# Applying the norm weights inside the high/low split of x, and squaring x on ScalarE

## The chip, the cores and the metric

The kernel runs on one core of a Trainium2 chip. The metric is the device time of one execution in microseconds (us); the median of the runs is compared.

## The reference

One inference step of a decoder with two layers, for 256 prompt tokens and 8 x 8 sample tokens (320 tokens in all, D = 1024, F = 2816). Each layer is

```
x = x + 0.5 * SwiGLU_1(rms(x))
h = rms(x); z = h @ w_in                     # 40 blocks of 128 columns
A, B = two kinds of windowed attention over z and the caches
x = x + (sigmoid(gA) * (A @ w_branch_a) + sigmoid(gB) * (B @ w_branch_b)) @ w_out
x = x + 0.5 * SwiGLU_2(rms(x))

def _rms(x, g):
    y = x * rsqrt(mean(x * x, axis=-1) + 1e-6)
    return y * g
```

and a last `_rms` follows the second layer. So there are seven norms: six in front of matrix products and one at the end. Everything is float32; the outputs are y and the new K/V window buffers.

## The kernel before, in words

**Layout.** Activations lie transposed: 128 partitions by 320 tokens, and x has KD = 8 such chunks. A weight comes as a *unit*, 128 x 1024 floats (8 tiles of 128 x 128); there are 208 units in a layer.

**Precision.** Every float32 product is made of three matrix products. An operand is split in a high part (rounded to fp32r) and a low part (operand minus high part): `product()` (L635 to L641) issues `hi*whi`, `lo*whi`, `hi*wlo`. ScalarE makes `whi` with a Copy (L973, `round_unit`), VectorE makes `wlo` with a subtraction (L1146, `rest_unit`). The rings `raw`, `whi` and `wlo` hold four units each; SyncE loads a unit into `raw` when the `wlo` that used the slot four units earlier is done.

**Norm.** The products take x times the norm's weights, and 1/rms is multiplied in behind them. For each of the 8 chunks of x:

1. VectorE, `add_to_x` (L1174): adds the result of the matrix product in PSUM to the chunk; it signals `taken`.
2. VectorE, `scale_x` (L1160): `xg = x * gain`, a tensor_scalar into one of two buffers `xg`; it signals `xg_ready`.
3. ScalarE, `round_x` (L985): `xhi = Copy(xg)`; it signals `xhi_done`.
4. VectorE, `rest_x` (L1165): `xlo = xg - xhi`; it signals `xs_ready`, on which TensorE waits chunk by chunk.
5. GpSimd, `add_squares` (L1407, L1409): `sq = x * x`, `ssq = ssq + sq`.

When all 8 are summed, TensorE adds over the partitions with a matrix of ones (`sum_squares`, L646), ScalarE takes the root (L978, which needs a table load), VectorE the reciprocal (L1170).

**Order around it.** The order is written out by hand, engine by engine; every engine runs its own instructions strictly in that order, and semaphores join them. There are four places with such chunks:

- the *start*, where x comes in four transfers with the first four weight units between them (L1367 to L1379 for VectorE);
- the *down* stages of the four FFNs, where a chunk of x is finished once in four units (`down` in `ffn_vec`, `ffn_act`; `ffn_pool`);
- the *w_out* stage of the two mixers, where a chunk is finished with every unit (last loops of `mixer_vec`, `mixer_act`, `mixer_pool`); there, TensorE writes to two banks in turn and may start unit m when the sum into x of unit m - 2 is `taken`;
- behind each of them `first_units` (L648 to L664): TensorE multiplies two new units side by side with chunks 0 to 6, and `sum_squares` stands in it behind the tenth product (chunk 2 of the second unit); chunk 7 of both comes last.

In the w_out stage VectorE's loop for unit m is

```
dve.wait_ge(unit_used, L * NU + U_WO + m + RING + 1)
add_to_x(L, BK_WO + m % 2, m, R_WO + m, 1.0)
scale_x(L * 3 + 2, m, m % 2)
rest_unit(L, U_WO + 4, 0, 0, m, UT)
rest_x(L * 3 + 2, m, m % 2)
```

The buffers `xg` and `sq` serve the mixer too (as `zs` and `sh`), at other times.

Of the kernel before, what the change touches and what calls it, by code (L numbers as in the profile page):

```python
# [13 lines left out]
P = 128  # L14
# [258 lines left out]
def build(nc, a):  # L273
    ctx = ExitStack()
    with ctx:
# [13 lines left out]
        xg = sb("xg", [P, 2, TOK])  # L289
        xhi = sb("xhi", [P, KD, TOK], F32R)  # L290
        xlo = sb("xlo", [P, KD, TOK], F32R)
        sq = sb("sq", [P, TOK])
# [48 lines left out]
        zs, sh = xg, sq  # L341
# [18 lines left out]
        xg_ready = sem("xg_ready")  # L360
# [607 lines left out]
        def _(act):  # L968
# [11 lines left out]

            def round_x(norm, m, slot):

                act.wait_ge(xg_ready, norm * KD + m + 1)
                dst = xhi[:, m, :] if isinstance(m, int) else xhi[:, at(m), :].rearrange("p o n -> p (o n)")
                nc.scalar.activation(dst, xg[:, slot, :], ACT.Copy).then_inc(xhi_done, 1)  # L985

            def ffn_act(L, f):
# [32 lines left out]
            def mixer_act(L):  # L1020
# [121 lines left out]
        def _(dve):  # L1142
# [16 lines left out]
            def scale_x(norm, m, slot):  # L1159
                nc.vector.tensor_scalar(xg[:, slot, :], chunk(x, m), gain(norm, m), None, ALU.mult)\  # L1160
                    .then_inc(xg_ready, 1)

            def rest_x(norm, m, slot):
                dve.wait_ge(xhi_done, norm * KD + m + 1)
                nc.vector.tensor_tensor(chunk(xlo, m), xg[:, slot, :], chunk(xhi, m).bitcast(F32), ALU.subtract)\  # L1165
                    .then_inc(xs_ready, 1)
# [11 lines left out]
            def ffn_vec(L, f):  # L1178
# [12 lines left out]
                def down(i, tail):  # L1191
                    norm = L * 3 + 1 + 2 * f
                    for o in range(2):
                        for s in range(4):
                            if s == 3:
                                dve.wait_ge(unit_used, L * NU + i * 8 + U_DN[f] + 4 * o + s + RING + 1)
                                add_to_x(L, BK_DN + o, i * 2 + o, i * 2 + R_DN[f] + o, 0.5)
                                scale_x(norm, i * 2 + o, o)
                            rest_unit(L, U_DN[f] + 4, i, 8, 4 * o + s,
                                      UT if o == 1 and tail == "next" else DN_TILES[s])  # L1200
                        rest_x(norm, i * 2 + o, o)
# [9 lines left out]
            def mixer_vec(L):  # L1211
# [158 lines left out]
            scale_x(0, 0, 0)  # L1370
            for m in range(KD):
                if m + 1 < KD:
                    dve.wait_ge(x_in[(m + 1) * XPARTS // KD], 16)
                    if m >= 1:
                        dve.wait_ge(xs_ready, m)
                    scale_x(0, m + 1, (m + 1) % 2)
# [180 lines left out]
```

## Time and profile before

| | |
|---|---|
| median of 3 runs | 1560.98 us (1560.46 to 1568.88) |
| profiled execution, first to last instruction | span 1556.9 us |
| busy: PE / DVE / ACT / POOL | 97% / 57% / 42% / 27% |
| chain that ended last | PE 87%, issue 4%, DVE 3%, DMA 3%, POOL 2%, ACT 1% |
| mean granted TensorE clock | 0.995 |

The profile gives the profiled execution by its span alone; the median of the runs stands 4.1 us above it. PE is TensorE, DVE VectorE, ACT ScalarE, POOL GpSimd. In a timeline a row is start, duration, engine, line, operation, output and inputs, shape and, in brackets, how long the engine had been idle and what ended that. A matmul's duration is its latency; how fast matmuls follow each other is read from their starts.

### The profile page before, as it was taken

How to read it: one execution, taken by the hardware profiler on the slowest of the kernel's cores; microseconds unless marked ns; L12 is line 12 of the kernel's file. 1: busy time of each engine (PE TensorE's matmuls, PEld its weight loads, DVE VectorE, ACT ScalarE, POOL GpSimd, SP SyncE). 2: the span in 40 equal slices, each digit the busy share in tenths (PEclk: the TensorE clock that was granted, in tenths of full speed). 3: DMA queues.
4: the chain of work that ended last, by engine and by line, in shares of the span. 5: the costliest groups of instructions: out<-in, count | busy, mean ns of one | idle time of the engine just before them, and what ended most of it. 6: DMA issues, size and time to landing. Idle time of an engine off the chain costs nothing.

```text
span 1556.9 us, 33517 instructions
## 1 busy us (share of the span) xinstructions
PE 1504.6 (97%) x11346; PEld 1425.1 (92%) x11346; DVE 883.5 (57%) x1383; ACT 656.7 (42%) x1123; POOL 414.7 (27%) x415
## 2 busy tenths in 40 slices
PE   6999999999999899999999999999999989999996
PEld 5999999988768899999999999999877689999996
DVE  7555567854334765555655455677534258545566
ACT  4444334455343344433344443355544344444333
POOL 5222223211113432222232222232111053322221
PEclk9999999999999999999999999999999999999998
DMA  7885565767685588646688846666776746985464
GB/s 283 323 298 187 169 202 192 254 205 246 216 283 170 175 312 295 217 149 187 203 307 296 287 141 190 206 222 206 244 254 228 244 139 219 326 303 160 145 202 159
DMA packets 95290, 352.11 MB, mean 226 GB/s; under 512 B 12368, under 2 KB 23888, under 8 KB 92496
## 3 DMA queue, kind: packets, MB, share of 16 engines
q1 hardware_dynamic: 95184, 350.77, 67.8%
q8 instruction: 58, 0.95, 0.2%
q14 instruction: 48, 0.39, 0.1%
HBM read 345.61 MB, written 94.37 MB: 283 GB/s over the span
## 4 chain that ended last, share of the span: by engine, by line
PE 87%; issue 4%; DVE 3%; DMA 3%; POOL 2%; ACT 1%; DVEq 0%; SPq 0%; POOLq 0%; ACTq 0%
PE ps L639 27%; PE ps L641 26%; PE ps L640 26%; PE ps L864 2%; DMA kvc<-in_kcache 2%; PE ps L850 2%; POOL ma L1460 1%; PE ps L723 1%; DMA kvc<-in_vcache 1%; DVE xlo L1165 1%; PE ps L791 1%; PE ps L758 1%; DVE wlo L1146 1%; PE ps L715 1%; DVE x L1174 0%
## 5 line engine op out<-in xcount | busy, mean ns | idle before, releaser
L1146 DVE TENSOR_TENSOR wlo<-raw,whi 128x1024 fp32r<-128x1024 f32 (+2 forms) x420 | 520.4, 1240 | 446.5 <-ACT whi L973 445.4
L639 PE MATMUL ps<-xhi,whi 128*128 128x320 f32 x2048 | 647.6, 316 | 16.3 <-DVE wlo L1146 8.4
L641 PE MATMUL ps<-xhi,wlo 128*128 128x320 f32 x2048 | 635.0, 310 | 0.0
L640 PE MATMUL ps<-xlo,whi 128*128 128x320 f32 x2048 | 634.8, 310 | 0.0
L973 ACT ACTIVATE whi<-raw 128x1024 fp32r<-128x1024 f32 (+2 forms) x420 | 403.8, 964 | 301.4 <-PE ps L641 301.2
L639 PEld LDWEIGHTS ps<-xhi,whi 128*128 128x128 f32 x2048 | 386.0, 188 | 39.2 <-issue 27.2
L640 PEld LDWEIGHTS ps<-xlo,whi 128*128 128x128 f32 x2048 | 386.6, 189 | 0.6 <-issue 0.2
L641 PEld LDWEIGHTS ps<-xhi,wlo 128*128 128x128 f32 x2048 | 386.4, 189 | 0.0
L641 PE MATMUL ps<-act_hi,wlo 128*128 128x320 f32 x704 | 217.6, 309 | 0.0
L639 PE MATMUL ps<-act_hi,whi 128*128 128x320 f32 x704 | 217.6, 309 | 0.0
L640 PE MATMUL ps<-act_lo,whi 128*128 128x320 f32 x704 | 217.6, 309 | 0.0
L1416 POOL TENSOR_TENSOR up_s<-gate_s,up_s 128x320 f32<-128x320 f32 x88 | 85.9, 976 | 379.6 <-DVE up_s L1187 379.6
L640 PEld LDWEIGHTS ps<-act_lo,whi 128*128 128x128 f32 x704 | 132.2, 188 | 0.0
L639 PEld LDWEIGHTS ps<-act_hi,whi 128*128 128x128 f32 x704 | 132.1, 188 | 0.0
L641 PEld LDWEIGHTS ps<-act_hi,wlo 128*128 128x128 f32 x704 | 132.1, 188 | 0.0
L1407 POOL TENSOR_TENSOR sq<-x 128x320 f32 (+1 forms) x56 | 44.7, 798 | 278.9 <-DVE x L1174 274.8
L1455 POOL TENSOR_TENSOR t<-xg,rinv 128x320 f32<-128x320 f32 x46 | 41.3, 897 | 261.8 <-ACT xg L1032 261.8
L994 ACT ACTIVATE gate_s<-gate_s 128x320 f32<-128x320 f32 x88 | 41.4, 470 | 164.0 <-DVE gate_s L1187 164.0
L1420 POOL TENSOR_TENSOR act_lo<-up_s,act_hi 128x320 f32 x88 | 86.5, 983 | 70.0 <-ACT act_hi L1002 70.0
L1032 ACT ACTIVATE xg<-ps 128x320 f32<-128x320 f32 x80 | 34.7, 434 | 142.8 <-PE ps L641 142.8
L1187 DVE TENSOR_TENSOR gate_s<-ps,rinv 128x320 f32<-128x320 f32 x88 | 43.2, 491 | 86.5 <-PE ps L641 85.9
L1064 ACT ACTIVATE e<-e,nmx 128x128 f32<-128x128 f32 (+5 forms) x60 | 32.9, 549 | 96.9 <-DVE nmx L1313 96.9
(123 smaller groups left out, 1362.7 us busy)
## 6 DMA issues: line engine op xcount, KB each, us to landing
out_new_a_sample<-in_cache_a SPq DMA_DIRECT2D x128, 510.0 KB, 5.7
raw<-in_ffn_gate SPq DMA_DIRECT2D x90, 512.0 KB, 3.9
raw<-in_ffn_up SPq DMA_DIRECT2D x90, 512.0 KB, 5.2
raw<-in_w_in SPq DMA_DIRECT2D x80, 512.0 KB, 4.3
kvc<-in_kcache SPq DMA_DIRECT2D x52, 512.0 KB, 5.5
kvc<-in_vcache SPq DMA_DIRECT2D x52, 512.0 KB, 4.5
raw<-in_ffn_down SPq DMA_DIRECT2D x64, 384.0 KB, 3.2
raw<-in_ffn_down SPq DMA_DIRECT2D x64, 320.0 KB, 3.0
```

Of the source, the lines that this page charges most:

```text
L639: pe.matmul(out, w0, hi, start=first, stop=False)
L640: pe.matmul(out, w0, lo, start=False, stop=False)
L641: return pe.matmul(out, w1, hi, start=False, stop=last)
L973: nc.scalar.activation(whi[:, (base + s) % RING, 0:tiles * P], raw[:, (base + s) % RAW, 0:tiles * P], ACT.Copy).then_inc(whi_done, 1)
L994: nc.scalar.activation(gate_s[:, s // 2, :], gate_s[:, s // 2, :], ACT.Silu)\
L1032: nc.scalar.activation(zs[:, n % 2, :], ps[:, n % 2, 0:TOK], ACT.Copy).then_inc(zs_done, 1)
L1146: nc.vector.tensor_tensor(wlo[:, (base + s) % RING, 0:tiles * P], raw[:, (base + s) % RAW, 0:tiles * P], whi[:, (base + s) % RING, 0:tiles ...
L1187: nc.vector.tensor_tensor((gate_s, up_s)[s % 2][:, s // 2, :], ps[:, s, 0:TOK], rinv[:, :], ALU.mult).then_inc(taken, 1)
L1407: nc.gpsimd.tensor_tensor(sq[:, :], chunk(x, m), chunk(x, m), ALU.mult).then_inc(sq_done, 1)
L1416: nc.gpsimd.tensor_tensor(up_s[:, q, :], gate_s[:, q, :], up_s[:, q, :], ALU.mult)\
L1420: nc.gpsimd.tensor_tensor(chunk(act_lo, j), up_s[:, q, :], chunk(act_hi, j).bitcast(F32), ALU.subtract).then_inc(actlo_done, 1)
L1455: nc.gpsimd.tensor_tensor(t1[:, n % 2, :], zs[:, n % 2, :], by[:, :], ALU.mult).then_inc(t1_done, 1)
```

## The change

ScalarE now makes `xhi` straight from x, with the norm's weights as the scale of its Copy. VectorE makes `xlo` as `x * gain - xhi` in a single scalar_tensor_tensor. `scale_x` and the buffer `xg` are gone. The square of x is a ScalarE Square into one of two buffers, directly behind the Copy; GpSimd only adds. The waits move with them: ScalarE waits for `taken` itself (or for x and the weights to land, at the start), and its Square of chunk m waits until GpSimd has added chunk m - 2.

```
-        xg = sb("xg", [P, 2, TOK])
+        zs = sb("zs", [P, 2, TOK])
-        sq = sb("sq", [P, TOK])
+        sq = sb("sq", [P, 2, TOK])
...
             def round_x(norm, m, slot):
-                act.wait_ge(xg_ready, norm * KD + m + 1)
-                dst = xhi[:, m, :] if isinstance(m, int) else xhi[:, at(m), :].rearrange("p o n -> p (o n)")
-                nc.scalar.activation(dst, xg[:, slot, :], ACT.Copy).then_inc(xhi_done, 1)
+                nc.scalar.activation(chunk(xhi, m), chunk(x, m), ACT.Copy, scale=gain(norm, m)).then_inc(xhi_done, 1)
+                act.wait_ge(ssq_done, norm * (KD + 1) + m)
+                plain(act)
+                nc.scalar.activation(sq[:, slot, :], chunk(x, m), ACT.Square).then_inc(sq_done, 1)
...
+                        act.wait_ge(taken, L * NR + i * 2 + R_DN[f] + o + RING + 1)
                         round_x(L * 3 + 1 + 2 * f, i * 2 + o, o)
...
                     round_unit(L, U_WO + 4, 0, 0, m, UT)
+                    act.wait_ge(taken, L * NR + R_WO + m + RING + 1)
                     round_x(L * 3 + 2, m, m % 2)
+            act.wait_ge(gains_in, 16)
             for m in range(KD):
+                act.wait_ge(x_in[m * XPARTS // KD], 16)
                 round_x(0, m, m % 2)
...
-            def scale_x(norm, m, slot):
-                nc.vector.tensor_scalar(xg[:, slot, :], chunk(x, m), gain(norm, m), None, ALU.mult)\
-                    .then_inc(xg_ready, 1)
-            def rest_x(norm, m, slot):
+            def rest_x(norm, m):
                 dve.wait_ge(xhi_done, norm * KD + m + 1)
-                nc.vector.tensor_tensor(chunk(xlo, m), xg[:, slot, :], chunk(xhi, m).bitcast(F32), ALU.subtract)\
-                    .then_inc(xs_ready, 1)
+                nc.vector.scalar_tensor_tensor(chunk(xlo, m), chunk(x, m), gain(norm, m), chunk(xhi, m).bitcast(F32),
+                                               ALU.mult, ALU.subtract).then_inc(xs_ready, 1)
...
                     add_to_x(L, BK_WO + m % 2, m, R_WO + m, 1.0)
-                    scale_x(L * 3 + 2, m, m % 2)
                     rest_unit(L, U_WO + 4, 0, 0, m, UT)
-                    rest_x(L * 3 + 2, m, m % 2)
+                    rest_x(L * 3 + 2, m)
...
-            def add_squares(norm, m):
+            def add_squares(norm, m, slot):
                 pool.wait_ge(ssq_done, norm * (KD + 1) + m + 1)
-                nc.gpsimd.tensor_tensor(sq[:, :], chunk(x, m), chunk(x, m), ALU.mult).then_inc(sq_done, 1)
                 pool.wait_ge(sq_done, norm * KD + m + 1)
-                nc.gpsimd.tensor_tensor(ssq[:, :], ssq[:, :], sq[:, :], ALU.add).then_inc(ssq_done, 1)
+                nc.gpsimd.tensor_tensor(ssq[:, :], ssq[:, :], sq[:, slot, :], ALU.add).then_inc(ssq_done, 1)
```

The `scale_x` call in `down` goes likewise, as do the two in the loop of the start.

ScalarE at the start of the program, before:

```order
L985 ACT_TABLE_LOAD
L985 ACTIVATE xhi<-xg 128x320 [waits xg_ready]
L973 ACTIVATE whi<-raw 128x1024 [waits raw_in0,unit_used]
L985 ACTIVATE xhi<-xg 128x320 [waits xg_ready] x3
L973 ACTIVATE whi<-raw 128x1024 [waits raw_in1,unit_used]
L985 ACTIVATE xhi<-xg 128x320 [waits xg_ready] x3
L973 ACTIVATE whi<-raw 128x1024 [waits raw_in2,unit_used]
```

and now:

```order
L991 ACT_TABLE_LOAD [waits x_in0]
L991 ACTIVATE xhi<-x,gains 128x320 [waits gains_in]
L994 ACTIVATE sq<-x 128x320 [waits ssq_done]
L972 ACTIVATE whi<-raw 128x1024 [waits raw_in0,unit_used]
L991 ACTIVATE xhi<-x,gains 128x320 [waits x_in0]
L994 ACTIVATE sq<-x 128x320 [waits ssq_done]
L991 ACTIVATE xhi<-x,gains 128x320 [waits x_in1]
L994 ACTIVATE sq<-x 128x320 [waits ssq_done]
```

The table load now stands behind the wait for the first part of x, and a Square stands behind every Copy, ahead of the weight unit's Copy. The whole program has 8 table loads in ScalarE's list before and after.

VectorE at the start, before:

```order
L1160 TENSOR_SCALAR xg<-x,gains 128x320 [waits x_in0,gains_in]
L1160 TENSOR_SCALAR xg<-x,gains 128x320 [waits x_in0]
L1165 TENSOR_TENSOR xlo<-xg,xhi 128x320 [waits xhi_done]
L1146 TENSOR_TENSOR wlo<-raw,whi 128x1024 [waits whi_done]
L1160 TENSOR_SCALAR xg<-x,gains 128x320 [waits xs_ready,x_in1]
L1165 TENSOR_TENSOR xlo<-xg,xhi 128x320 [waits xhi_done]
```

and now:

```order
L1174 SCALAR_TENSOR_TENSOR xlo<-x,gains,xhi 128x320 [waits x_in0,xhi_done,gains_in]
L1159 TENSOR_TENSOR wlo<-raw,whi 128x1024 [waits whi_done]
L1174 SCALAR_TENSOR_TENSOR xlo<-x,gains,xhi 128x320 [waits xhi_done,x_in0]
L1174 SCALAR_TENSOR_TENSOR xlo<-x,gains,xhi 128x320 [waits xhi_done,x_in1] x2
L1159 TENSOR_TENSOR wlo<-raw,whi 128x1024 [waits whi_done]
```

Eight instructions of 128 x 320 are left where sixteen were, and the four `wlo` stand among them as before.

VectorE in the w_out stage, one unit (L1174 is `add_to_x` before; now it is L1183), before:

```order
L1174 SCALAR_TENSOR_TENSOR x<-ps,x 128x320 [waits unit_used]
L1176 REGISTER_ALU
L1160 ISA [waits taken]
L1160 TENSOR_SCALAR xg<-x,gains 128x320
L1146 TENSOR_TENSOR wlo<-raw,whi 128x1024 [waits whi_done]
L1164 REGISTER_ALU
L1165 TENSOR_TENSOR xlo<-xg,xhi 128x320 [waits xhi_done]
```

and now:

```order
L1183 SCALAR_TENSOR_TENSOR x<-ps,x 128x320 [waits unit_used]
L1185 REGISTER_ALU
L1159 TENSOR_TENSOR wlo<-raw,whi 128x1024 [waits whi_done,taken]
L1173 ISA
L1174 ISA [waits xhi_done]
L1174 SCALAR_TENSOR_TENSOR xlo<-x,gains,xhi 128x320
```

The tensor_scalar is gone from between the sum and the weight unit's low part; the rest keeps its order.

## Rows read from the trace of the kernel before

**Rows 1.** The page: busy time of each engine.
```profile
PE 1504.6 (97%) x11346; PEld 1425.1 (92%) x11346; DVE 883.5 (57%) x1383; ACT 656.7 (42%) x1123; POOL 414.7 (27%) x415
```
**Rows 2.** Waits of TensorE: us in total, times, longest.
```profile
PE ps L639 <- DVE xlo L1165: 5.8, 7, 1.8
PE ps L646 <- POOL ssq L1409: 3.9, 3, 3.5
```
**Rows 3.** Timeline of the start, VectorE.
```profile
9.57 0.65 DVE L1160 TENSOR_SCALAR xg<-x,gains 128x320 f32<-128x320 f32 x1
10.15 1.18 DVE L1165 TENSOR_TENSOR xlo<-xg,xhi 128x320 fp32r<-128x320 f32 x1
11.44 0.65 DVE L1160 TENSOR_SCALAR xg<-x,gains 128x320 f32<-128x320 f32 x1
```
**Rows 4.** Timeline of the start, TensorE.
```profile
8.42 0.63 PE L639 MATMUL ps<-xhi,whi 128*128 128x320 f32 x1 [8.42 <-DVE wlo L1146]
...
19.95 0.63 PE L639 MATMUL ps<-xhi,whi 128*128 128x320 f32 x1 [0.70 <-DVE xlo L1165]
...
24.84 0.31 PE L641 MATMUL ps<-xhi,wlo 128*128 128x320 f32 x1
...
27.19 0.31 PE L639 MATMUL ps<-xhi,whi 128*128 128x320 f32 x1
```
**Rows 5.** Timeline of the start, ScalarE, then GpSimd.
```profile
0.75 1.28 ACT L985 ACT_TABLE_LOAD   x1 [0.75 <-PEq L1548]
5.85 1.06 ACT L973 ACTIVATE whi<-raw 128x1024 fp32r<-128x1024 f32 x1 [0.21 <-DMA raw<-in_ffn_gate]
...
4.23 0.72 POOL L1407 TENSOR_TENSOR sq<-x 128x320 f32<-128x320 f32 x1 [3.12 <-DMA x<-in_x]
...
10.12 0.86 POOL L1409 TENSOR_TENSOR ssq<-ssq,sq 128x320 f32<-128x320 f32 x1
```
**Rows 6.** Timeline of the first w_out stage, VectorE, unit 1 of 8.
```profile
527.28 0.48 DVE L1174 SCALAR_TENSOR_TENSOR x<-ps,x 128x320 f32<-128x320 f32 x1
527.90 0.92 DVE L1160 TENSOR_SCALAR xg<-x,gains 128x320 f32<-128x320 f32 x1
528.74 1.94 DVE L1146 TENSOR_TENSOR wlo<-raw,whi 128x1024 fp32r<-128x1024 f32 x1
530.60 0.48 DVE L1165 TENSOR_TENSOR xlo<-xg,xhi 128x320 fp32r<-128x320 f32 x1
```
**Rows 7.** Timeline of TensorE there: two units' first matmuls, then the FFN's first units.
```profile
527.81 0.41 PE L639 MATMUL ps<-mhi,whi 128*128 128x320 f32 x1
...
531.53 0.41 PE L639 MATMUL ps<-mhi,whi 128*128 128x320 f32 x1
...
549.73 0.41 PE L639 MATMUL ps<-xhi,whi 128*128 128x320 f32 x1 [0.62 <-DVE xlo L1165]
...
551.97 0.81 PE L646 MATMUL ps<-ssq,ones 128*128 128x320 f32 x2 [0.21 <-POOL ssq L1409]
```
**Rows 8.** Groups by line and shape, whole trace: count, busy, mean ns, idle before.
```profile
L1389 DVE SCALAR_TENSOR_TENSOR x<-x,gains,rinv 128x320 f32<-128x320 f32 x8 | 3.8, 547 | 0.0
L978 ACT ACTIVATE rms<-ps,eps 128x320 f32<-128x320 f32 x7 | 3.7, 527 | 9.0 <-PE ps L646 8.9
```
**Rows 9.** Timeline of the last norm: ScalarE, VectorE, GpSimd.
```profile
1543.15 1.06 ACT L973 ACTIVATE whi<-raw 128x1024 fp32r<-128x1024 f32 x1 [1.14 <-PE ps L641]
...
1544.24 1.61 DVE L1146 TENSOR_TENSOR wlo<-raw,whi 128x1024 fp32r<-128x1024 f32 x1
...
1544.85 1.72 POOL L1409 TENSOR_TENSOR ssq<-ssq,sq 128x320 f32<-128x320 f32 x1
```
**Rows 10.** Timeline at the end of the first FFN: GpSimd, then TensorE.
```profile
254.37 1.75 POOL L1409 TENSOR_TENSOR ssq<-ssq,sq 128x320 f32<-128x320 f32 x1
...
256.87 0.70 PE L646 MATMUL ps<-ssq,ones 128*128 128x320 f32 x2
```
**Rows 11.** A stretch of 5 us; granted TensorE clock behind POOL's busy time.
```profile
515.00:520.00 5.00, 4.90 (x23) 4.90 (x24) 1.25 (x2) 0.47 (x1) 3.00 (x4) 0.66 0.65 206
```

More of the change, by code:

```diff
@@ L340, in build @@
         qm = qm_mem[:, 0:4 * N_QM * 6 * NT].rearrange("p (b j n) -> p b j n", b=4, j=N_QM)
-        zs, sh = xg, sq
+        sh = sq[:, 0, :]
         pm = qm_mem[:, :].rearrange("p (f b i n) -> p f b i n", f=2, b=4, i=CT)
@@ L359, in build @@
         actlo_done = sem("actlo_done")
-        xg_ready = sem("xg_ready")
         xhi_done = sem("xhi_done")
@@ L979, in root, with chunk, gain @@
                     .then_inc(rms_done, 1)
+            def chunk(t, m):
+                return t[:, m, :] if isinstance(m, int) else t[:, at(m), :].rearrange("p o n -> p (o n)")
+            def gain(norm, m):
+                if isinstance(norm, int) and isinstance(m, int):
+                    return gains[:, norm, m:m + 1]
+                g = gains[:, :, :].rearrange("p n k -> p (n k)")
+                return g[:, at(norm * KD + m)]
             def round_x(norm, m, slot):
-                act.wait_ge(xg_ready, norm * KD + m + 1)
-                dst = xhi[:, m, :] if isinstance(m, int) else xhi[:, at(m), :].rearrange("p o n -> p (o n)")
-                nc.scalar.activation(dst, xg[:, slot, :], ACT.Copy).then_inc(xhi_done, 1)
+                nc.scalar.activation(chunk(xhi, m), chunk(x, m), ACT.Copy, scale=gain(norm, m)).then_inc(xhi_done, 1)
+                act.wait_ge(ssq_done, norm * (KD + 1) + m)
+                plain(act)
+                nc.scalar.activation(sq[:, slot, :], chunk(x, m), ACT.Square).then_inc(sq_done, 1)
             def ffn_act(L, f):
@@ L1197, in down @@
                                 add_to_x(L, BK_DN + o, i * 2 + o, i * 2 + R_DN[f] + o, 0.5)
-                                scale_x(norm, i * 2 + o, o)
                             rest_unit(L, U_DN[f] + 4, i, 8, 4 * o + s,
                                       UT if o == 1 and tail == "next" else DN_TILES[s])
-                        rest_x(norm, i * 2 + o, o)
+                        rest_x(norm, i * 2 + o)
                 gate_up(0, True, (UT,) * 4)
@@ L1369, in _ @@
             dve.wait_ge(x_in[0], 16)
-            scale_x(0, 0, 0)
             for m in range(KD):
[L1372 to L1376, printed above, removed]
-                rest_x(0, m, m % 2)
+                dve.wait_ge(x_in[m * XPARTS // KD], 16)
+                rest_x(0, m)
                 if m in START_UNITS:
@@ L1425, in ffn_pool @@
                     for o in range(2):
-                        pool.wait_ge(taken, L * NR + i * 2 + R_DN[f] + o + RING + 1)
-                        add_squares(norm, i * 2 + o)
+                        add_squares(norm, i * 2 + o, o)
             def mixer_pool(L):
@@ L1466, in mixer_pool @@
                 for m in range(KD):
-                    pool.wait_ge(taken, L * NR + R_WO + m + RING + 1)
-                    add_squares(norm, m)
+                    add_squares(norm, m, m % 2)
             clear_squares(0, True)
             for m in range(KD):
-                pool.wait_ge(x_in[m * XPARTS // KD], 16)
-                add_squares(0, m)
+                add_squares(0, m, m % 2)
             with pool.Fori(0, DEPTH) as L:
```

## The prediction

> **What bounds the kernel now.** The page comes first: TensorE is busy 97% of the span, the other engines 57%, 42% and 27% [rows 1]. An average can't say what VectorE, ScalarE or GpSimd work is worth, so the list of TensorE's waits is next: only 5.8 us of waits for `xlo` and 3.9 us for the sum of squares touch this change, 3.5 us of the latter a single wait in the last norm [rows 2]. Everything else that the change edits lies beside matrix products. Where waits end last is then read from three timelines.
>
> At the start, TensorE's first matmul comes at 8.42 us, the matmul on chunk 6 only at 19.95, after the last of the waits for `xlo`; from there it needs 7.24 us until both units are done and the third begins at 27.19 [rows 4]. VectorE is what it waits for: its pair of tensor_scalar and `xlo` repeats every 1.87 us (9.57 to 11.44), and `xlo` takes 1.18 us where the same subtraction takes 0.48 elsewhere [rows 3, 6]. Beside it stands GpSimd's addition, 10.12 to 10.98 [rows 5]: the two engines hold each other up, `xlo` ends 0.35 us behind it. TensorE's pace says something too: the last 16 matmuls before 27.19 start every 0.147 us (24.84 to 27.19), while the 16 instructions from 19.95 to 24.84 take 0.31 us each [rows 4]: that is 2.4 GHz against 1.2 GHz, reached after five us without a pause.
>
> In the w_out stage TensorE's units start 3.72 us apart (527.81, 531.53) [rows 7], though 24 matmuls at 0.147 us take 3.53. The list of waits hardly shows it, since each is too short. VectorE shows it: sum to scale 0.62 us, scale to `wlo` 0.84, `wlo` to `xlo` 1.86, and 0.40 more to the next sum make 3.72, without idle time [rows 6]. The scale and `wlo` are both stretched by GpSimd's two operations. So in this stage VectorE is the bound, by 0.2 us a unit, and behind it the chunks come late to the FFN's first units: waits of 0.62 and 0.21 us [rows 7].
>
> **The sum, part by part.** Changes are counted in the profiled execution's span, 1556.9 us, and carried over to the median, 1560.98, which stands 4.1 us above it.
>
> *1. The start, about -2.8 us.* The table load ran at 0.75 us, hidden by the transfers; now it waits for x, which lands at 4.23 [rows 5], and ends at 5.51. The Copy takes 0.48 to 0.56 us (0.47 as shown for Copies of this size; a per-partition operand may add up to the 0.53 of the root, which has one [rows 8]), the Square about 0.47, so the first weight unit's Copy starts at some 6.4 us, not 5.85 [rows 5], and the first matmul at 8.9. From there, before: 11.53 us to chunk 6, of which 1.1 is the one `wlo` between, so 1.74 us a chunk. After: VectorE has one operation of 0.48 us a chunk and GpSimd one of 0.86. If they don't hinder each other GpSimd's own 0.86 and a handover of 0.14 make 1.0; if they take strict turns it is 0.86 + 0.48 = 1.34. I take 1.2: `xlo` needed 0.35 us behind GpSimd's end, not 0.48. 6 x 1.2 + 1.1 = 8.3: chunk 6 at 17.2 in place of 19.95, 2.8 earlier (1.9 to 3.9 between the two ends). The 7.24 us behind it stay, if the clock rises as long after the last pause as before.
>
> The Trainium skill, SBUF — State Buffer, section "Who interferes with whom", says that the port pair that VectorE and GpSimd share is an exclusive lock held for the whole instruction. By that the pace would be 1.34, the start's gain 1.9 and the time 1554.5. The trace shows the exclusion, but also that part of the loser's time runs under the winner's.
>
> *2. The two w_out stages, about -4.4 us.* VectorE loses the tensor_scalar and its 0.84 us: 3.72 - 0.84 = 2.88 us a unit [rows 6], even if `wlo` stays stretched. GpSimd has one operation a chunk left, so only one of `wlo` and `xlo` can be held up by it. ScalarE needs 1.05 + 0.56 + 0.47 = 2.1 us a unit. Both are under 3.53, so TensorE sets the pace. From unit 3 to the sum of squares there are 150 matmuls: 150 x 0.147 = 22.05 us, against 24.16 (527.81 to 551.97) [rows 7]; with the step from unit 2 to 3 the excess is 2.3. I take 2.2 a layer, since units 0 and 1 end together and VectorE starts with a unit in arrears. What is late next? After the last unit ScalarE does the unit's Copy (1.05), Copy (0.56) and Square (0.47), GpSimd adds (0.86, and at worst 0.8 behind a `wlo`): 3.7 us, and TensorE comes to the sum of squares after 30 matmuls, 4.4 us. So neither wait comes back.
>
> *3. The four down stages, 0.* A chunk comes every four units, 9.7 us. At the first FFN's end GpSimd's sum ends at 256.12, the matrix of ones is reached at 256.87 without waiting [rows 10]. Now the Square runs after the Copy, but GpSimd's own multiplication is gone: the sum comes at about the same time. If it were to come 1 us later, 0.25 us a norm would show, 1 us in all.
>
> *4. The last norm, about -0.2 us.* Nothing covers it. Before: the sum ends at 1546.57 (1544.85 + 1.72), held up by a `wlo` that runs to 1545.85 [rows 9]. After: ScalarE's unit Copy ends at 1544.21, Copy to 1544.7, Square to 1545.15; `wlo` of 1544.24, now not delayed, ends near 1545.5, and 0.86 us later, at 1546.35, the sum is there. If VectorE's `xlo` gets in first it is 1546.8, so -0.3 to +0.2.
>
> *5. ScalarE's 56 Squares (56 x 0.47 = 26 us) and 56 fewer operations each on VectorE and GpSimd elsewhere: 0*, hidden by TensorE. The list of instructions shows no additional table load.
>
> Sum: -2.8 - 4.4 - 0.2 = -7.4, so 1553.6 us, 0.47% faster. About 0.5% (7.8 us) is what a measurement of this kernel tells from no change, so the forecast lies right at that border.
>
> **The rivals.**
>
> *A. The start gives nothing* (w_out as above): 1560.98 - 4.6 = 1556.4. For it: the Square stands before the unit's Copy, and waits for GpSimd's addition two chunks back, so ScalarE, VectorE and GpSimd form a ring. Or `xlo` itself is slow: at twice the 0.47 us of the rows, 6 x 0.47 = 2.8 us are gone again; w_out's 2.88 + 0.47 = 3.35 still fits. Against it: eight scalar_tensor_tensors with two operands in SBUF and a per-partition one took 3.8 us, 0.47 each back to back [rows 8]. The Trainium skill, Vector Engine (DVE) Microarchitecture Reference, section "Points that are easy to get wrong", says that this kind of instruction with two SBUF sources that aren't bf16 runs at half throughput; by this rule A holds, and the trace disagrees.
>
> *B. Only the start pays*: VectorE's loop was not the bound in w_out, or a unit in arrears stays so. 1560.98 - 3.0 = 1558.0. Against it: VectorE had no idle time there at all.
>
> *C. The clock rises earlier.* With a chunk every 1.2 us, 0.8 of which is three slow matmuls, TensorE pauses less from 8.9 us on. If it runs at 2.4 GHz by chunk 6, 30 matmuls and the sum of squares take some 5 us, not 7.24: another -2.3, so 1551.3. Against: one longer pause remains, behind the second `wlo`.
>
> *D. A stretch of low clock moves.* Behind a wait TensorE had a granted clock of 0.66 over 515 to 520 [rows 11], about 3.4 us at the lower level, costing 1.7. Whether such a stretch falls in after a wait may change with 7 us of shift; two more give 1557.0.
>
> *E. Slower.* At the start GpSimd's addition, held up by `xlo` and `wlo`, delays the Square two chunks on, which delays the next Copy, so the next `xlo`: a ring of about 0.86 + 1.18, or 2.04 us a chunk. It decides from a pace of 1.74 on. Price: 0.5 (table load and Square first) + 6 x 0.3 = 2.3; if in w_out `xlo` then takes 1.18 as well, and the sum waits on it, 2.88 + 0.7 = 3.6, which gives back what was gained there, and an additional low stretch of clock costs 1.7. 1560.98 + 4.0 = 1565.0. Against: at the start GpSimd needs one operation a chunk, not two.
>
> That the change does something else than it says is ruled out by the list of instructions.
>
> **How the numbers follow.** The forecast 0.56, A 0.15, B 0.08, C 0.12, D 0.05, E 0.04. The range runs from 1550.8, a little past C, to 1558.5, past B; it leaves out E and the ends of the others. Faster by over 0.5% (below 1553.2): C, and a little under half of the forecast's own spread (1552.2 to 1555.0), 0.12 + 0.26 = 0.38. Slower by over 0.5% (above 1568.8): the far end of E and what I haven't thought of, 0.03. The rest, 0.59, is within.
>
> **What would show it.** Right: w_out units 3.53 us apart on TensorE, VectorE idle there, the waits of 0.62 and 0.21 gone; the matmul on chunk 6 at about 17.2 and the third unit at about 24.4; first ScalarE Copy at 5.5; `xlo` near 0.48 or 1.2 and never a steady 0.9; the last norm's sum at TensorE 0.2 us sooner behind the last product. Wrong: a pace of 3.7 in w_out (B), chunk 6 at 19 us or later (A, E), matmuls 0.147 us apart before 21 us (C), more stretches of granted clock under 1 (D).

## The result, and the profile after

The changed kernel took 1551.41 us (median of 5 runs, 1550.20 to 1551.68) against 1561.21 for the kernel before beside it (5 runs, 1560.46 to 1568.88): ratio 0.9934, 95% interval 0.9914 to 0.9955. A second comparison, of more runs, gave 1555.22 (11 runs, 1551.87 to 1559.69) against 1560.34 (23 runs, 1556.32 to 1565.69): 0.9967, interval 0.9955 to 0.9979 (the runs of e6_after_again below). So the gain is 9.8 us by the first and 5.1 by the second; the forecast of 1553.6, 7.4 below, lies between them and 2.3 to 2.4 us from either. The change is faster, by an amount at the border of the 0.5%.

The profiled execution spans 1549.1 us, and its own time was 1550.88: a time is the span and 1.8 us. By that the profiled execution of before (1556.9) took about 1558.7, so of the 4.1 us between its span and the median only 1.8 is fixed; the rest is that this execution was a quick one.

The page after, and TensorE's longest waits that concern the change or stand out:

```profile
PE 1501.6 (97%) x11346; PEld 1426.1 (92%) x11346; DVE 822.8 (53%) x1327; ACT 681.4 (44%) x1179; POOL 361.6 (23%) x359
```
```profile
PE ps L638 <- DVE wlo L1159: 12.2, 2, 9.2
...
PE ps L645 <- POOL ssq L1410: 3.2, 1, 3.2
...
PE ps L638 <- DVE xlo L1174: 1.0, 1, 1.0
```

Against [rows 1] VectorE is 61 us less busy, GpSimd 53 us less, ScalarE 25 us more; that is no gain by itself, as TensorE was busy 97% before and is now. Against [rows 2] the seven waits for `xlo` (5.8 us) have shrunk to one of 1.0, and of the three for the sum of squares only the last norm's is left. The wait of 9.2 us for `wlo` is the kernel's first matmul; the other one, 2.9, is the pause between the layers, on which more below.

**Where the time went** is read from the times of fixed points: the starts of TensorE's sums of squares and of VectorE's first sum into x in w_out. The second execution of each kernel is from e9_before_again and e6_after_again below.

| starts at | before | before, second | after | after, second |
|---|---|---|---|---|
| sum of squares at the start | 23.31 | 23.64 | 19.53 | 19.74 |
| the same, end of first FFN | 256.87 | 257.27 | 252.39 | 253.22 |
| first w_out chunk added, layer 1 | 523.53 | 523.79 | 518.51 | 520.00 |
| sum of squares behind it | 551.97 | 552.23 | 544.68 | 546.17 |
| end of layer 1's second FFN | 787.05 | 789.27 | 782.23 | 783.47 |
| end of layer 2's first FFN | 1019.91 | 1022.12 | 1015.10 | 1016.33 |
| first w_out chunk added, layer 2 | 1285.96 | 1289.72 | 1280.31 | 1285.71 |
| sum of squares behind it | 1314.40 | 1318.18 | 1306.49 | 1311.88 |
| sum of squares, last norm | 1546.62 | 1550.40 | 1538.30 | 1543.70 |

Two stages gain in both pairs alike: from the start to the end of the first FFN (4.5 and 4.1 us) and w_out (28.4 before and 26.2 after, in both layers and both executions). The rest scatters: from the first FFN's end in layer 2 to w_out it took 266.1 and 267.6 us before, 265.2 and 269.4 after, though the change touches nothing there.

**The start.** Timelines after: ScalarE from its first instruction, then VectorE, GpSimd and TensorE (rows with "x3" are three instructions in a row; their time covers all three).

```profile
4.57 1.28 ACT L991 ACT_TABLE_LOAD   x1 [4.57 <-DMA x<-in_x]
5.87 0.56 ACT L991 ACTIVATE xhi<-x,gains 128x320 fp32r<-128x320 f32 x1
6.33 0.45 ACT L994 ACTIVATE sq<-x 128x320 f32<-128x320 f32 x1
6.69 1.04 ACT L972 ACTIVATE whi<-raw 128x1024 fp32r<-128x1024 f32 x1
```
```profile
8.91 3.30 DVE L1174 SCALAR_TENSOR_TENSOR xlo<-x,gains,xhi 128x320 fp32r<-128x320 f32 x3
```
```profile
8.69 3.17 POOL L1410 TENSOR_TENSOR ssq<-ssq,sq 128x320 f32<-128x320 f32 x3 [0.84 <-ACT sq L994]
```
```profile
9.25 0.63 PE L638 MATMUL ps<-xhi,whi 128*128 128x320 f32 x1 [9.25 <-DVE wlo L1159]
...
14.47 0.63 PE L638 MATMUL ps<-xhi,whi 128*128 128x320 f32 x1 [1.03 <-DVE xlo L1174]
...
15.54 0.64 PE L638 MATMUL ps<-xhi,whi 128*128 128x320 f32 x1
...
16.62 0.63 PE L638 MATMUL ps<-xhi,whi 128*128 128x320 f32 x1
...
19.09 0.30 PE L638 MATMUL ps<-xhi,whi 128*128 128x320 f32 x1
...
19.53 0.70 PE L645 MATMUL ps<-ssq,ones 128*128 128x320 f32 x2
```

The table load is no longer hidden, and the first matmul comes 0.8 us later than in [rows 4]. From there a chunk takes 1.08 us (15.54 to 16.62): VectorE's three `xlo` take 3.30 us and GpSimd's three additions beside them 3.17, so the two engines run in step at 1.1 us a chunk. Chunk 6 comes at 16.62, not 19.95. At 19.09 a matmul takes 0.30 us: the granted clock has risen at 19.0 us, where before it rose at 24.7, 1.4 us behind the sum of squares. The third unit begins at 22.71 (27.19 before). The early rise isn't there in every execution. In the second one chunk 6 comes at 16.38, the sum of squares at 19.74 at half clock still, and the third unit at 23.54; in the second of before they are 20.27, 23.64 and 27.59:

```profile
16.38 0.64 PE L638 MATMUL ps<-xhi,whi 128*128 128x320 f32 x1
...
19.74 1.27 PE L645 MATMUL ps<-ssq,ones 128*128 128x320 f32 x2
...
23.54 0.31 PE L638 MATMUL ps<-xhi,whi 128*128 128x320 f32 x1
```

**w_out.** VectorE after, unit 1 and the next sum; then TensorE, units 2 and 3:

```profile
521.99 0.48 DVE L1183 SCALAR_TENSOR_TENSOR x<-ps,x 128x320 f32<-128x320 f32 x1
522.50 1.23 DVE L1159 TENSOR_TENSOR wlo<-raw,whi 128x1024 fp32r<-128x1024 f32 x1
523.64 1.20 DVE L1174 SCALAR_TENSOR_TENSOR xlo<-x,gains,xhi 128x320 fp32r<-128x320 f32 x1
524.77 0.48 DVE L1183 SCALAR_TENSOR_TENSOR x<-ps,x 128x320 f32<-128x320 f32 x1
```
```profile
525.32 0.31 PE L638 MATMUL ps<-mhi,whi 128*128 128x320 f32 x1
...
528.84 0.31 PE L638 MATMUL ps<-mhi,whi 128*128 128x320 f32 x1
...
544.68 0.70 PE L645 MATMUL ps<-ssq,ones 128*128 128x320 f32 x2
```

VectorE's loop has gone from 3.72 us [rows 6] to 2.78, and TensorE's units stand 3.52 apart. Once VectorE has caught up, from unit 4 on, it is the one that waits for `whi`, 0.38 us and then 0.67 a unit. `wlo` is short now (1.23, not 1.94), and `xlo` is the one that is held up (1.20, not 0.48).

**The last norm.**

```profile
1536.31 1.22 DVE L1159 TENSOR_TENSOR wlo<-raw,whi 128x1024 fp32r<-128x1024 f32 x1 [0.64 <-ACT whi L972]
```
```profile
1537.09 1.15 POOL L1410 TENSOR_TENSOR ssq<-ssq,sq 128x320 f32<-128x320 f32 x1 [8.76 <-ACT sq L994]
```
```profile
1538.30 1.43 PE L645 MATMUL ps<-ssq,ones 128*128 128x320 f32 x2 [3.19 <-POOL ssq L1410]
```

And before:

```profile
1546.62 1.01 PE L646 MATMUL ps<-ssq,ones 128*128 128x320 f32 x2 [3.50 <-POOL ssq L1409]
```

The addition takes 1.15 us, not 1.72 [rows 9], and TensorE's wait is 3.19, not 3.50. But the clock has fallen to half by then and the matmul takes 1.43 us, against 1.01 before: the 0.3 is more than given back. From the start of the last product to the end of the span it is 14.12 us before and 14.26 after (second executions: 14.01 and 14.26).

### The profile page after: what moved, and what is told of

It is laid out like the page before. It is cut to its first block, busy times and chain, and to the rows that moved or that the text cites. A ratio compares the mean times of both kernels' runs of the same rounds, so it can differ in the third digit from the quotient of the medians.

```text
span 1549.1 us, 33560 instructions
## 1 busy us (share of the span) xinstructions
PE 1501.6 (97%) x11346; PEld 1426.1 (92%) x11346; DVE 822.8 (53%) x1327; ACT 681.4 (44%) x1179; POOL 361.6 (23%) x359
## 4 chain that ended last, share of the span: by engine, by line
PE 86%; issue 6%; DMA 3%; POOL 3%; DVE 1%; ACT 1%; POOLq 0%; SPq 0%; DVEq 0%; ACTq 0%
PE ps L638 26%; PE ps L640 25%; PE ps L639 25%; DMA kvc<-in_kcache 2%; PE ps L849 2%; PE ps L863 2%; POOL ma L1460 1%; DMA kvc<-in_vcache 1%; PE ps L722 1%; PE ps L790 1%; PE ps L757 1%; PE ps L714 1%; POOL ssq L1410 1%; POOL mlo L1463 0%; PE ps L780 0%
## 5 line engine op out<-in xcount | busy, mean ns | idle before, releaser
L1159 DVE TENSOR_TENSOR wlo<-raw,whi 128x1024 fp32r<-128x1024 f32 (+2 forms) x420 | 492.3, 1173 | 497.0 <-ACT whi L972 496.6
L1410 POOL TENSOR_TENSOR ssq<-ssq,sq 128x320 f32<-128x320 f32 x56 | 60.5, 1081 | 325.2 <-ACT sq L994 324.9
L1455 POOL TENSOR_TENSOR t<-zs,rinv 128x320 f32<-128x320 f32 x46 | 41.2, 896 | 259.2 <-ACT zs L1042 259.2
L1042 ACT ACTIVATE zs<-ps 128x320 f32<-128x320 f32 x80 | 34.7, 434 | 140.4 <-PE ps L640 140.4
```

What stands on the lines that cost most here:

```text
L1042: nc.scalar.activation(zs[:, n % 2, :], ps[:, n % 2, 0:TOK], ACT.Copy).then_inc(zs_done, 1)
L1159: nc.vector.tensor_tensor(wlo[:, (base + s) % RING, 0:tiles * P], raw[:, (base + s) % RAW, 0:tiles * P], whi[:, (base + s) % RING, 0:tiles ...
L1410: nc.gpsimd.tensor_tensor(ssq[:, :], ssq[:, :], sq[:, slot, :], ALU.add).then_inc(ssq_done, 1)
L1455: nc.gpsimd.tensor_tensor(t1[:, n % 2, :], zs[:, n % 2, :], by[:, :], ALU.mult).then_inc(t1_done, 1)
```

## The experiments

Theory T is the prediction's: the gain comes at the start and in w_out because VectorE, held up by GpSimd, was late there, and nowhere else. Its rivals are that one half of the change does all of it, or that the gain sits elsewhere. A second question came from the first profile: TensorE's pause at the step from layer 1 to layer 2 (where the loop starts again and the next weights are not ready). Before and after:

```profile
782.55 0.41 PE L639 MATMUL ps<-xhi,whi 128*128 128x320 f32 x1 [1.86 <-issue]
```
```profile
776.21 0.41 PE L638 MATMUL ps<-xhi,whi 128*128 128x320 f32 x1 [2.92 <-DVE wlo L1159]
```

The idle time is 1.86 us before, 2.92 after. Counted from the start of the last product to that of the next, as the expectations do, it is 2.17 and 3.23. Theory F puts the longer pause down to the moment at which cache copies and instruction fetches meet, theory G to a longer list of instructions on ScalarE.

Timed runs. The first four were run beside 35 runs of the kernel before (1560.66), the last four beside 23 (1560.34). The profiled executions e9 to e11 are single runs and have no interval.

| | median | ratio to before, 95% |
|---|---|---|
| e1_fold_only | 1557.33 | 0.9976 (0.9962 to 0.9989) |
| e2_square_only | 1554.85 | 0.9961 (0.9949 to 0.9973) |
| e3_old_start | 1558.71 | 0.9981 (0.9968 to 0.9995) |
| e5_old_wout | 1557.63 | 0.9986 (0.9971 to 1.0002) |
| e4_early_table | 1553.79 | 0.9952 (0.9934 to 0.9971) |
| e6_after_again | 1555.22 | 0.9967 (0.9955 to 0.9979) |
| e7_copy_later | 1555.84 | 0.9967 (0.9953 to 0.9981) |
| e8_all_three | 1554.97 | 0.9960 (0.9945 to 0.9974) |

The intervals overlap so much that these times don't tell the variants apart: e2 with half of the change is at the whole change's ratio, and e1, e3 and e5 stand 1.4 to 3 us above it, e5 not clear of the kernel before. What follows rests on the fixed points in the traces.

**e1_fold_only: only the weights move; GpSimd squares.** Edit to the changed kernel:

```
-                act.wait_ge(ssq_done, norm * (KD + 1) + m)
-                plain(act)
-                nc.scalar.activation(sq[:, slot, :], chunk(x, m), ACT.Square).then_inc(sq_done, 1)
...
+                nc.gpsimd.tensor_tensor(sq[:, slot, :], chunk(x, m), chunk(x, m), ALU.mult).then_inc(sq_done, 1)
```

> Only the fold of the weights (scaled Copy on ScalarE, scalar_tensor_tensor on VectorE); the squares stay on GpSimd. Theory T (two places pay: the start, where VectorE and GpSimd hold each other up, and w_out, where VectorE alone was over TensorE's 3.53 us a unit; either half of the change brings w_out under 3.53): w_out units 3.53 us apart, 2.2 us a layer; at the start xlo is no longer paced by the scale, but the sum of squares still ends near 22 us, so only 1 to 2 us are gained there: 1555.0 us. Rival R (the gain belongs to the fold alone, the Squares give nothing): 1551.4 us, as the whole change.

Measured: w_out 26.18 and 26.16 us from first sum to sum of squares, so the fold alone has the whole gain there. At the start chunk 6 comes at 17.25, but the sum of squares only at 23.31, as before:

```profile
23.31 0.90 PE L645 MATMUL ps<-ssq,ones 128*128 128x320 f32 x1 [2.86 <-POOL ssq L1408]
```

The wait for `xlo` has become one for GpSimd, which has two operations a chunk. Without the Squares on ScalarE, the start gains nothing, where 1 to 2 us were expected. Behind that wait the clock is at half again and the third unit begins at 28.14, 0.95 later than before (27.19).

**e2_square_only: only the Square moves; VectorE keeps the tensor_scalar** (the Square behind the Copy as now):

```
-                nc.scalar.activation(chunk(xhi, m), chunk(x, m), ACT.Copy, scale=gain(norm, m)).then_inc(xhi_done, 1)
+                act.wait_ge(xg_ready, norm * KD + m + 1)
...
+                nc.scalar.activation(dst, xg[:, slot, :], ACT.Copy).then_inc(xhi_done, 1)
...
+            def scale_x(norm, m, slot):
+                nc.vector.tensor_scalar(xg[:, slot, :], chunk(x, m), gain(norm, m), None, ALU.mult)\
+                    .then_inc(xg_ready, 1)
```

> Only the Square on ScalarE; xg, the tensor_scalar and the tensor_tensor stay on VectorE. Theory T: in w_out VectorE needs 0.62 + 0.39 + 1.14 + 1.1 = 3.25 us a unit, under 3.53, so units are 3.53 us apart and 2.2 us a layer are gained; at the start a chunk takes about 1.55 us, not 1.87: 1.5 to 2 us. 1555.0 us. Rival R (the fold alone pays): units stay 3.72 us apart and the time 1561.2 us.

Measured: chunk 6 at 18.04, the sum of squares at 21.34, 2.0 us before 23.31. In w_out VectorE's loop takes 3.15 us:

```profile
524.35 0.48 DVE L1178 SCALAR_TENSOR_TENSOR x<-ps,x 128x320 f32<-128x320 f32 x1
524.97 0.39 DVE L1164 TENSOR_SCALAR xg<-x,gains 128x320 f32<-128x320 f32 x1
525.27 1.22 DVE L1150 TENSOR_TENSOR wlo<-raw,whi 128x1024 fp32r<-128x1024 f32 x1
526.41 1.18 DVE L1169 TENSOR_TENSOR xlo<-xg,xhi 128x320 fp32r<-128x320 f32 x1
527.51 0.48 DVE L1178 SCALAR_TENSOR_TENSOR x<-ps,x 128x320 f32<-128x320 f32 x1
```

3.15 is under TensorE's 3.52, and the stage takes 26.18 again. So either half is enough in w_out, and the second adds nothing there. The tensor_scalar has 0.39 us of its own; the 0.92 of [rows 6] was more than half GpSimd.

**e3_old_start: all of the change, but the start as before** (tensor_scalar, subtraction and GpSimd's two operations for norm 0):

```
-                round_x(0, m, m % 2)
+                act.wait_ge(xg_ready, m + 1)
+                nc.scalar.activation(xhi[:, m, :], xg[:, m % 2, :], ACT.Copy).then_inc(xhi_done, 1)
...
-                rest_x(0, m)
...
+                    scale_start(m + 1)
...
+                nc.vector.tensor_tensor(xlo[:, m, :], xg[:, m % 2, :], xhi[:, m, :].bitcast(F32), ALU.subtract)\
+                    .then_inc(xs_ready, 1)
...
+                nc.gpsimd.tensor_tensor(sq[:, 0, :], x[:, m, :], x[:, m, :], ALU.mult).then_inc(sq_done, 1)
```

> The whole change, but the start of the program as before (scale on VectorE, squares on GpSimd). Theory T: the matmul on chunk 6 at 19.95 us again, all that the start gave is lost (3.8 us up to the sum of squares, 0.7 more behind it by the clock): 1551.4 + 4.5 = 1555.9 us. Rival (the start's lead is lost again later, in waits for transfers of the first FFN or the mixer): 1551.4 to 1552.5 us.

Measured: chunk 6 at 20.50, sum of squares at 23.87, VectorE's pairs 1.87 us apart again; w_out 26.16. The start's gain is gone and only that.

**e5_old_wout: all of the change, but w_out as before**, on all three engines; VectorE's part:

```
+                    nc.vector.tensor_scalar(xg[:, m % 2, :], x[:, m, :], gain(L * 3 + 2, m), None, ALU.mult)\
+                        .then_inc(xg_ready, 1)
...
-                    rest_x(L * 3 + 2, m)
...
+                    nc.vector.tensor_tensor(xlo[:, m, :], xg[:, m % 2, :], xhi[:, m, :].bitcast(F32), ALU.subtract)\
+                        .then_inc(xs_ready, 1)
```

> The whole change, but the w_out stages as before. Theory T: units 3.72 us apart again, waits of 0.6 and 0.2 us in the FFN's first units are back, 2.3 us a layer: 1551.4 + 4.5 = 1555.9 us. Rival (the gain in the middle came from fewer stretches of low clock and shorter waits for cache loads, not from w_out): 1551.4 to 1553 us.

Measured: w_out 28.45 and 28.47, the sums into x 3.72 us apart; the start as in the changed kernel (16.60, 19.96).

```profile
522.92 0.48 DVE L1185 SCALAR_TENSOR_TENSOR x<-ps,x 128x320 f32<-128x320 f32 x1
523.54 0.92 DVE L1367 TENSOR_SCALAR zs<-x,gains 128x320 f32<-128x320 f32 x1
524.38 1.93 DVE L1161 TENSOR_TENSOR wlo<-raw,whi 128x1024 fp32r<-128x1024 f32 x1
526.24 0.48 DVE L1371 TENSOR_TENSOR xlo<-zs,xhi 128x320 fp32r<-128x320 f32 x1
526.64 0.48 DVE L1185 SCALAR_TENSOR_TENSOR x<-ps,x 128x320 f32<-128x320 f32 x1
```

This is [rows 6] within 0.01 us. With e3 it places the gain: in each of the two the edited stage loses its own part, and the other keeps its own. The times give back less than the traces: 1555.9 was expected of both, from 1551.4 and 4.5, but beside the second median of the changed kernel (0.9967) e3 is 2.2 us slower and e5 3.0. Five of e5's twelve runs lie at 1561.5 to 1563.9, the profiled one among them; it has four half-clock stretches of 6.8 us.

**e4_early_table: a Copy of one column ahead of the wait for x**, so that the table is loaded early.

```
+            act.wait_ge(set_up, 2)
+            nc.scalar.activation(rms[:, 0:1], eps[:, :], ACT.Copy)
             act.wait_ge(gains_in, 16)
```

> The whole change, with a Copy of one column ahead of ScalarE's wait for x, so that the table load runs at 1 us again and not behind the transfer. If the table load is what sets the start: first Copy at 4.6 in place of 5.87 us, first matmul at 8.4 in place of 9.25, chunk 6 up to 0.9 us sooner (15.7), 0.5 to 1 us less in all. Rival (the arrival of x and of the second weight unit sets it): first matmul sooner, chunk 6 at 16.6 as before, and the time unchanged.

Measured: the table load is at 0.75 again and the first Copy at 4.57:

```profile
0.75 1.28 ACT L1141 ACT_TABLE_LOAD   x1 [0.75 <-PEq L1548]
...
4.57 0.56 ACT L991 ACTIVATE xhi<-x,gains 128x320 fp32r<-128x320 f32 x1 [2.33 <-DMA x<-in_x]
```

First matmul 8.44 (9.25 in the changed kernel), chunk 6 at 15.82. But the sum of squares comes at 19.19, only 0.3 to 0.6 us sooner, and at the first FFN's end it is 252.38 against 252.39 and 253.22: the 0.8 us at the first matmul is not seen there. 1553.79 is the lowest median of this set, yet its interval overlaps that of the unaltered change.

**e6_after_again: the changed kernel once more**, beside those variants.

> The changed kernel again, unchanged, beside the others on the same chip. Expected 1551 to 1553 us. At the step from layer 1 to layer 2 TensorE pauses 2.9 us again and a stretch of low clock follows; elsewhere the stretches of low clock and the waits for cache loads may fall otherwise than in the first trace.

Measured: 1555.22, above the 1551 to 1553 expected, with runs over 7.8 us; the profiled one spans 1554.5, 5.4 more than the first. The pause between the layers is 2.97. Its start (16.38, 19.74) and w_out (26.17 twice) agree with the first. The difference lies elsewhere, and about 3 us of it can be pointed at. Two 5 us windows of this execution, then the same windows of before (the third column from the right is the granted clock):

```profile
1145.00:1150.00 5.00, 3.20 (x34) 2.33 (x30) 1.51 (x3) 0.84 (x3) 0.00 (x0) 0.74 0.98 346
1150.00:1155.00 5.00, 5.00 (x33) 4.37 (x33) 1.41 (x5) 0.71 (x2) 0.00 (x0) 0.58 0.32 117
```
```profile
1145.00:1150.00 5.00, 4.20 (x59) 3.20 (x55) 2.97 (x8) 3.42 (x7) 0.87 (x1) 1.00 0.79 242
1150.00:1155.00 5.00, 4.21 (x51) 3.50 (x52) 1.51 (x6) 0.71 (x2) 0.00 (x0) 1.00 0.97 376
```

Such stretches at half clock (1.2 GHz) last 3.4 or 6.8 us; in them matmuls start 0.27 us apart, not 0.147, so 3.4 us of one cost about 1.5 where TensorE is busy. Between the start and the last norm the first profile of before has two (6.8 us in all), the first of after three (10.2), the second executions of both 17.1 each: 6.8 us more of it than in the first of after, at most 3.1 us of time.

**e7_copy_later: SyncE issues layer 2's first cache copies one group later**, to test F.

```
+                if f == 0:
+                    group(first, None)
+                    first += 1
```

> The whole change, but in the first FFN of a layer the copies of the large cache begin one group of four units later. Theory F: TensorE's pause at the step between layers is its instruction fetch, a DMA that queues behind the cache copies; SyncE now issues its second copy 0.14 us before TensorE comes there, not 1.0 us after. Without copies there the pause falls from 3.1 us to under 2, no stretch of low clock follows: 2.5 to 3 us less than the same kernel beside it. Rival G (the pause grew because ScalarE's program is longer by the Squares): pause and time unchanged.

Measured: 2.67 us instead of 3.23 and 2.97, not the under 2 that F called for; no half-clock stretch behind it, and no gain in time (1555.84, where F called for 2.5 to 3 us).

**e8_all_three: the early table, the later copy, and at the start the unit's Copy ahead of the Square.**

> The whole change with three edits: the early table load, the later copies, and at the start the weight unit's Copy ahead of the Square of the same chunk. If all hold: first matmul at 8.0 us, the pause between the layers under 2 us, 3.5 us less than the changed kernel beside it. If only the later copies hold: 2.5 to 3 us less, as that kernel alone.

Measured: start 15.88 and 19.24, as e4; pause 2.47, but with a half-clock stretch at 778.3; 1554.97. The first matmul is at 8.49, where 8.0 was expected, and the pause not under 2: neither expectation came in, and the time is that of the changed kernel.

**e9_before_again: the kernel before, unchanged, profiled again.**

> The kernel before, unchanged, profiled once more. It is the control for the pause of TensorE at the step from layer 1 to layer 2, which was 2.17 us in the first profile of it and 2.7 to 3.2 us in every kernel in which ScalarE squares x (fold only: 1.89). Both theories (F: the pause grows because transfers and instruction fetches meet at another moment, since SyncE issues the cache copies earlier against TensorE; G: it grows because ScalarE's program in the layer loop is longer) expect 2.0 +- 0.25 us here and no half-clock stretch behind it. If it is 2.6 us or more, the pause just scatters from run to run and neither is needed. The half-clock stretches elsewhere may fall otherwise than in the first profile (390, 516, 1547); w_out from the first sum to the sum of squares stays 28.45.

Measured: a pause of 2.78 us, and a half-clock stretch behind it. Rows at the step, and the windows behind it here and in the first profile of before:

```profile
783.42 0.63 PE L639 MATMUL ps<-xhi,whi 128*128 128x320 f32 x1 [2.48 <-issue]
```
```profile
783.00:788.00 5.00, 4.58 (x22) 4.58 (x23) 1.75 (x2) 1.28 (x1) 1.41 (x1) 0.66 1.03 376
```
```profile
780.00:785.00 5.00, 3.14 (x22) 2.88 (x21) 4.32 (x5) 1.53 (x2) 2.52 (x2) 1.00 1.08 359
```

The same program gives 2.17 with no stretch and 2.78 with one. It took 1562.42 us here, and another run of it on the same chip 1565.95. By the expectation's own words the pause scatters, and neither F nor G is needed for values up to there.

**e10_padded_fold: e1 with four empty semaphore increments behind each Copy**, which makes ScalarE's list longer.

```
                 nc.scalar.activation(chunk(xhi, m), chunk(x, m), ACT.Copy, scale=gain(norm, m)).then_inc(xhi_done, 1)
+                plain(act)
+                plain(act)
+                plain(act)
+                plain(act)
```

> Fold only (e1_fold_only) with four empty semaphore increments behind each Copy of x on ScalarE: ScalarE's list in the layer loop is then as long as or longer than in the changed kernel, but it has no Square and costs next to no time (4 x about 0.05 us a chunk). G: the pause at the layer step goes from 1.9 to 2.7 us or more, and a half-clock stretch follows it. F: it stays 1.9 +- 0.25. w_out 26.2 in both.

Measured: 3.21 us with a half-clock stretch at 787.1 behind it (e1: 1.89, none). One run, 1566.03, beside 1565.95 for before.

**e11_down_on_pool: the change, but GpSimd squares x in the down stages.**

```
-                        round_x(L * 3 + 1 + 2 * f, i * 2 + o, o)
+                        round_x(L * 3 + 1 + 2 * f, i * 2 + o, o, False)
...
+                        nc.gpsimd.tensor_tensor(sq[:, o, :], chunk(x, i * 2 + o), chunk(x, i * 2 + o), ALU.mult).then_inc(sq_done, 1)
```

> The changed kernel, but in the down stages GpSimd squares x again; start and w_out keep the Square on ScalarE. At the layer step the last down stage of layer 1 is then as in fold only, and ScalarE's list is longer than there by the w_out Squares alone. F (timing at the end of the down stage): the pause is 1.9 +- 0.25 us. G (length of ScalarE's list): between fold only's 1.9 and the change's 3.0, some 2.4. If it stays at 2.9 or more, neither the down Squares nor their length is the cause. The start (chunk 6 at about 16.6) and w_out (26.2) as in the changed kernel; the first FFN's sum of squares without a wait.

Measured: 3.15 us and a stretch at 782.0; start 16.30 and 19.67, w_out 26.17 twice. One run, 1556.09. F called for 1.9, G for 2.4. That speaks against the Squares of the down stages as the cause, as far as one execution can. Putting them back costs the first FFN's end nothing (253.09).

**What of the pause is settled.** Kernels with the short list on ScalarE had 1.89, 2.17 and 2.78 us; those with Squares or padding, ten profiles, 2.47 to 3.23. F's value came in none of e7, e10 and e11. The direction is G's, e10 gives the value that G asked for, e11 does not, and two executions of one kernel lie 0.6 apart. The cause stays open. If the change does lengthen the pause, it is by about 0.7 us in the mean of these profiles. What comes behind it weighs more. From w_out's sum of squares in layer 1 to the next one it takes 234.7 to 235.5 us in the three profiles without a half-clock stretch there (before, e1, e7) and 236.8 to 238.7 in the ten with one. Nine of the ten profiles with the longer list have it, one of the other three. That the change makes it likelier isn't shown by so few, but it would be a loss of some 2 us that the prediction has nowhere.

## Why the prediction was right, and where it was off

*1. The start.* Predicted -2.8 (1.9 to 3.9), measured -3.3 at chunk 6, -3.8 at the sum of squares and -4.5 at the third unit and the first FFN's end. In the second pair it is -3.9, -3.9 and, at those two, -4.1. The mechanism holds (e3), but the term was undersized, and both totals lie outside its own bounds. The pace was taken as 1.2 us a chunk and is 1.08: the addition and `xlo` overlap more than the 0.35 us taken over from before. From the first matmul to chunk 6 it takes 7.37 and 7.39 us (11.53 and 11.54 before), where 8.3 was worked out: that is 0.9 us of the difference, in both pairs.

"The 7.24 us behind it stay" very nearly holds, but not in the first profile of the change. Chunk 6 to the third unit takes 6.09 there, as the clock rose at 19.0, and 7.16 in its second execution; in the variants with the new start (e4, e5, e7, e8, e11) it takes 6.81 to 7.15, and before 7.24 and 7.32. So rival C's sign, matmuls 0.147 us apart before 21 us, is there in the first profile, with half of C's price (1.15 us, not 2.3), and isn't there in the second execution of the same program. That the first median, 1551.41, lies at C's 1551.3 is no evidence for C. The prediction also sets 0.31 us a matmul against 0.147 as the two levels of the clock; its 0.31 is an average with the sum of squares in it, and matmuls at 1.2 GHz start 0.27 us apart.

The first matmul came at 9.25, where 8.9 was predicted: the load ended 0.35 us later than worked out. In the second execution it came at 8.99.

The Trainium skill's rule of an exclusive lock (SBUF — State Buffer, "Who interferes with whom") would give 1.34 a chunk. The trace shows 1.08: behind the first one `xlo` is always held up, 1.1 us long where a plain subtraction has 0.48, yet the two instructions take turns in less than the sum of their times. The rule gives the direction and not the price.

*2. w_out.* Predicted -2.2 a layer, measured -2.27 (28.44 to 26.17); VectorE's loop predicted 2.88 and measured 2.78. TensorE's pace of 3.53 is there (3.52), the waits of 0.62 and 0.21 are gone, and only one of `wlo` and `xlo` is held up, as said. What the prediction didn't see is that moving the Square alone would do (e2): `wlo`'s step falls from 1.86 to 1.14 us, `xlo`'s grows from 0.40 to 1.10, and what remains as gain is the tensor_scalar's, from 0.84 to 0.30.

*3. Down stages.* 0 predicted; no wait for `xlo` or the sum of squares there. At the first FFN's end GpSimd's sum ends 1.08 us ahead of the matrix of ones (250.14 + 1.17, and 252.39), where it was 0.75 before.

*4. Last norm.* -0.2 predicted, -0.3 at the matmul. But that matmul runs at half clock (+0.4), and from the last product to the end it takes 0.14 and 0.25 us longer: in both pairs the term has the wrong sign. In e3, e4 and e8, with the same last norm, the clock falls later (the matmul takes 0.81 to 0.87 us) and from the last product to the end it takes 13.6 to 13.7 us, 0.4 to 0.5 less than before. The prediction's sum has no word on when the clock falls there, and that outweighs the 0.3.

*5. The rest.* 0 predicted. Between the stages the first pair lost 2.5 us in the two FFNs between 551.97 and 1019.91 (467.94 before, 470.42 after) and won 1.4 in the mixers; the second pair lost 2.0 in the mixers and 0.3 in those FFNs. Before itself differs by 1.9 there (469.89 in its second execution). This is rival D as scatter, in both kernels: the sign that it named, more stretches of low clock, is there in the first pair (three, not two) and not in the second (four and four).

The stage terms add up to 8.9 us in the first pair and 8.4 in the second, where 7.4 was forecast, and the spans differ by 7.9 and 6.1. So the forecast came out near the measured times in part by luck: the start was undersized by 1.3 to 1.7 us, and what was lost between the stages, put at nothing, covered it. The first comparison (9.8) has more than the stages give; the second (5.1, interval 3.3 to 7.0) is below them, and what lies between is not attributed. Half-clock stretches, waits for cache loads and the pause move from run to run, and no run shows which of them the change makes likelier; the stretch behind the pause between the layers is the first to look at.

*Rival A* (a start that gives nothing, by the ring or a slow scalar_tensor_tensor) is refuted: chunk 6 came 3.3 and 3.9 us sooner, and where GpSimd seldom stands beside it `xlo` takes 0.55 us (the group of the down stages, below), with two float32 sources; a plain subtraction takes 0.48. The half-throughput rule of the Trainium skill (Vector Engine (DVE) Microarchitecture Reference, "Points that are easy to get wrong") doesn't show here.

```profile
L1174 DVE SCALAR_TENSOR_TENSOR xlo<-x,gains,xhi x24 | 13.2, 551 | 0.0
```

*B* is refuted by e5. *E* didn't occur: ring and contention leave the pace at 1.08, far from 1.74. The ring shows once: a Square at 14.18 waited 0.86 us for GpSimd's addition.

## What to carry to other kernels

Look for the stage where a helper engine has no idle time, not at its share of the whole: here 57% hid a loop that was 0.2 us a unit too slow for TensorE. Two ways of relieving such a loop don't add up once it is under the next bound, while at the start, where a chain of three engines sets the pace, the fold alone gave nothing at the sum of squares, the Square alone 2.0 us and both together 3.8. And when a stage gain is a few us of 1560, judge it by fixed points in two traces of each kernel: two comparisons of medians gave 9.8 and 5.1 us.

## What was not expected of the hardware

- An operation that GpSimd holds up is stretched, not just delayed: on VectorE in w_out `wlo` took 1.94 us and `xlo` 0.48 before (again in e5), 1.23 and 1.17 to 1.20 after, steady within 0.03 us from unit to unit. In e1, where GpSimd's operations fall otherwise, `wlo` took 1.23 to 1.61 and `xlo` 1.00 to 1.17. Which of them it hits depends on where GpSimd's operation falls.
- The granted clock fell to half for 3.4 or 6.8 us in places that differ between two executions of one program: three stretches and four in the two profiles of the change, of which only two stand at the same place (at the pause ahead of w_out, 510.5 and 512.5, and at the layer step, 776.7 and 778.8).
- A ScalarE Copy with a per-partition scale took 0.55 us against 0.47 without.
- Waits placed ahead of the first activation hold back its table load too: 1.28 us moved from 0.75 to 4.57 (e4 moves it back).
